# Four buffers of split weights moved to 0, 32, 64 and 192 bytes past a multiple of 256

## What is computed

```python
proj = jnp.einsum('bsd,dc->bsc', h, w_in)                    # first layer, 3420 columns
x = x + jnp.einsum('bsc,cd->bsd', mixed, w_out)
# two layers of the second kind
h = rms_norm_2(x) * (1 + sc_m) + sh_m
proj = h @ w_in                                              # 3520 columns
x = x + g_m * (y @ w_out)
gate, up = jnp.split(h @ w_ffn_in, 2, axis=-1)               # 1024 -> 2 x 2816
x = x + g_f * ((jax.nn.silu(gate) * up) @ w_ffn_out)         # 2816 -> 1024
```

## Time and profile before

| | |
|---|---|
| median of three runs | 1832.57 us |
| the profiled execution, whole | 1833.59 us |
| its span, first to last instruction | 1831.4 us |
| TensorE busy with matmuls | 1759.6 us (96%) |
| TensorE loading weights | 1424.0 us (78%) |
| VectorE, ScalarE, GpSimd busy | 965.0, 724.1, 686.1 us |
| mean granted TensorE clock | 0.988 |
| DMA, share of 16 engines | 31.4% |

### The profile page before, as it was taken

How to read it: one execution, slowest core, us unless ns; L and a number is a source line. 1 busy time by engine, 2 the same in 40 slices (tenths; PEclk the granted TensorE clock), 3 DMA queues, 4 the chain that set the end, 5 groups by cost and what they waited for, 6 DMA issues and landing times. The chain is left out here.

```text
span 1831.4 us, 23403 instructions
## 1 busy us (share of the span) xinstructions
PE 1759.6 (96%) x8343; PEld 1424.0 (78%) x8349; DVE 965.0 (53%) x1746; ACT 724.1 (40%) x1244; POOL 686.1 (37%) x303
## 2 busy tenths in 40 slices
PE   6999999988999999999999999999999999999997
PEld 6877777777888766788888887888766788888886
DVE  7989688575579577633333322579665321101112
ACT  5434555623375554332213222466454232213221
POOL 2424111235430333554555555450211454444442
PEclk9999999999999999999999999999999999999998
DMA  6234001044332224355555532232211233232211
GB/s 244 81 104 138 24 25 35 24 166 135 113 104 99 76 80 137 128 207 184 185 189 201 184 139 92 81 115 93 103 35 35 69 104 101 83 106 101 93 58 47
DMA packets 56634, 197.67 MB, mean 108 GB/s; under 512 B 6993, under 2 KB 8017, under 8 KB 56530
## 3 DMA queue, kind: packets, MB, share of 16 engines
q1 hardware_dynamic: 56530, 196.26, 31.4%
HBM read 194.14 MB, written 2.10 MB: 107 GB/s over the span
## 5 line engine op out<-in xcount | busy, mean ns | idle before, releaser
L496 POOL TENSOR_TENSOR WL<-RAW,WH 128x1024 fp32r<-128x1024 f32 x234 | 590.7, 2529 | 907.7 <-ACT WH L585 568.0
L1743 PE MATMUL bank<-HH,WH 128*128 128x512 f32 x1120 | 437.0, 390 | 7.8 <-POOLq L501 5.8
L1745 PE MATMUL bank<-HH,WL 128*128 128x512 f32 x1120 | 435.9, 389 | 0.0
L1744 PE MATMUL bank<-HL,WH 128*128 128x512 f32 x1120 | 435.8, 389 | 0.0
L585 ACT ACTIVATE WH<-RAW 128x1024 fp32r<-128x1024 f32 x259 | 270.6, 1051 | 243.1 <-PE bank L1745 218.0
L1743 PEld LDWEIGHTS bank<-HH,WH 128*128 128x128 f32 x1120 | 210.2, 188 | 53.5 <-issue 10.1
L1745 PEld LDWEIGHTS bank<-HH,WL 128*128 128x128 f32 x1120 | 210.2, 188 | 43.8
L1744 PEld LDWEIGHTS bank<-HL,WH 128*128 128x128 f32 x1120 | 210.3, 188 | 43.1
L1676 DVE TENSOR_TENSOR HF<-SILU,bank 128x512 f32<-128x512 f32 x44 | 30.3, 688 | 314.2 <-PE bank L1745 311.2
L1743 PE MATMUL bank<-HDH,WH 128*128 128x512 f32 x352 | 137.1, 389 | 0.0
L1745 PE MATMUL bank<-HDH,WL 128*128 128x512 f32 x352 | 136.9, 389 | 0.0
(11 more groups left out here) (363 smaller groups left out, 2871.1 us busy)
## 6 DMA issues: line engine op xcount, KB each, us to landing
RAW<-in_stream SPq DMA_DIRECT2D x363, 512.0 KB, 3.3
out_t<-YA SPq DMA_DIRECT2D x8, 256.0 KB, 2.2
X<-in_xt SPq DMA_DIRECT2D x3, 512.0 KB, 8.7
X<-in_xt SPq DMA_DIRECT2D x2, 256.0 KB, 3.9
RAW<-in_stream SPq DMA_DIRECT2D x2, 256.0 KB, 4.2
ACC<-in_pos SPq DMA_DIRECT2D x1, 256.0 KB
gains<-in_gains SPq DMA_DIRECT2D x1, 224.0 KB
CS<-in_cs SPq DMA_DIRECT2D x1, 128.0 KB
```

The source lines that it names most:

```text
L496: nc.gpsimd.tensor_tensor(lo(k)[:], raw(k)[:], hi(k)[:].bitcast(F32), ALU.subtract).then_inc(sem["passed"], mark("passed", *k))
L1743: nc.tensor.matmul(out, A[0], B[0], start=first, stop=False)
L1744: nc.tensor.matmul(out, A[0], B[1], start=False, stop=False)
L1745: return nc.tensor.matmul(out, A[1], B[0], start=False, stop=last)
```

## The change

The four buffers of `WH` and of `WL` are moved up by 0, 32, 64 and 192 bytes. The small constants behind them move up by 192. To make room, `ones` shrinks from 128 to 64 columns (only 64 are ever read), and its load shrinks with it; so `ident` lies 192 bytes further on and all that follows `ones` 64 bytes further down. `W0` is rounded up to a multiple of 256 and comes out at the same 108 KB + 7936 bytes as before. `X`, `HH`, `HL`, `RAW` and everything in the work area stay where they were. No instruction is added, removed or moved on any engine, and no wait changes; the one instruction that differs in shape is the load of `ones` (128x64 in place of 128x128).

```diff
 SPLIT_RING = 4
+RING_SHIFT = (0, 32, 64, 192)
...
-        WH = [at(f"WH{i}", [P, 1024], F32R, (split0 + 8 * i) * KB) for i in range(SPLIT_RING)]
-        WL = [at(f"WL{i}", [P, 1024], F32R, (split0 + 4 + 8 * i) * KB) for i in range(SPLIT_RING)]
-        cur = [(split0 + 8 * SPLIT_RING) * KB]
+        WH = [at(f"WH{i}", [P, 1024], F32R, (split0 + 8 * i) * KB + RING_SHIFT[i]) for i in range(SPLIT_RING)]
+        WL = [at(f"WL{i}", [P, 1024], F32R, (split0 + 4 + 8 * i) * KB + RING_SHIFT[i]) for i in range(SPLIT_RING)]
+        cur = [(split0 + 8 * SPLIT_RING) * KB + RING_SHIFT[-1]]
...
-        ones = small("ones", [P, P], F32)
+        ones = small("ones", [P, 2 * NCMP], F32)
...
-        W0 = (cur[0] + 63) // 64 * 64 + 128
+        W0 = (cur[0] + 255) // 256 * 256
...
-            for dst, name in ((ones, "ones"), (ident, "ident")):
-                sp.dma_start(dst[:], a[name]).then_inc(sem["norm_consts"], mark("norm_consts", by=16))
+            sp.dma_start(ones[:], a["ones"][:, 0:2 * NCMP]).then_inc(sem["norm_consts"], mark("norm_consts", by=16))
+            sp.dma_start(ident[:], a["ident"]).then_inc(sem["norm_consts"], mark("norm_consts", by=16))
```

## The result

The changed kernel takes 1853.5 us (median of four runs, 1853.3 to 1858.2) against 1832.6 before, 20.9 us more; the ratio is 1.0139 with a 95% interval of 1.0120 to 1.0159. So it is slower, by nearly twice what I had forecast (11.9 us), and inside the range. The profiled execution is one of 1853.5 us with a span of 1851.3.

The account below looks back on a forecast made before the run. TensorE's matmul pace was taken to bound the kernel. To the median of 1832.6 us, 11.9 us was added for re-settling at slot passages, all other parts 0, giving 1844.5 us; the 8-in-10 range was 1808 to 1866.

Parts of the forecast that it names:

- The bounds: Per matmul in the shifted buffers: at best 10 ns less, 44 us in all; at worst 9 ns more, 40 us.
- the 13.3 ns: Each fp32r matmul of 512 columns at full clock: time above the 213.3 ns that its columns alone take.
- If the pace has to settle again each time and then reaches 227: At each of 259 passages between weight slots: settling again costs 0.046 us, 11.9 us in all; chance 0.27.
- The third rival: Slower in shifted buffers: never settling, 4.6 ns a matmul, 1853 us, or one notch higher, 6.7 ns, 1862 us; chance 0.22.
- faster: In shifted buffers a distance avoids one encounter of both streams, saving 6.7 ns a matmul; 1803 to 1828 us; chance 0.28.
- same: The matmul surcharge arises whatever the distance between weight load and moving stream; time stays at 1832.6 us; chance 0.23.
- The prediction's second place: The skill's rule for the distance of matmuls at full clock, N/2.4 + 2.5 ns, 215.8 here.

## Why the prediction was wrong

What bounds the kernel was read rightly: TensorE's pace went to the end, 22.7 us busy for 19.9 us of span, and the suppliers had room.

The bounds were right: the worst settled pace (234.3) and the best (226.7) lie inside the -10 to +9 ns taken from the earlier trace rows. That the pace depends on how weight load and stream lie to each other was right too. Whether the 13.3 ns that are left at distance 0 also come from that is not shown.

The step that failed is "If the pace has to settle again each time and then reaches 227". I read in the earlier trace rows that the pace is a settled state with an approach, and took it for granted that every distance has the same settled state. That put the change of the settled pace at nothing without a row for it. It is not nothing: with all buffers at 64, where nothing is left to settle, it is 233.3. And the approach itself was sized too large: 46 ns was the one at the start of a stage, behind matmuls of another kind; at a passage it is 30 ns into buffer 0 and 8 on average. Two errors of opposite sign: 2.1 us in place of 11.9 for the passages, and 23.0 in place of 0 for the settled paces. The third rival had it nearly whole, "settles one notch higher", 6.7 ns; its sum of 1862 took all three buffers at that notch, and buffer 3 is at a third of it. That its other sum, 1853 for a pace that never settles, is the measured time is luck: every buffer settles. Nor was the forecast the likeliest case by its own chances (0.27 against 0.28 for faster); it stood between the others.

The rival "same" falls with the all-64 kernel, and "faster" with the list of offsets: of the eight tried, 0 is the best at 512 columns. Its argument, that streams which start together at equal offsets must collide more, has the sign wrong there. The argument for a notch higher ("all paces on the way in but one or two are above 227") was the best evidence in the trace, and I should have given it more than 0.22: it says that 227 is at the low end of the paces seen, reached at one distance, and no row showed that another distance has it too.

The Trainium skill's page "SBUF — State Buffer", section "Who interferes with whom", has TensorE wait for nobody and its two read ports independent. The runs differ: moving the weights by 64 against the stream costs 6.7 ns a matmul, moving both costs nothing. No row speaks against the rule between engines (the dense windows of the earlier trace rows keep their pace at DMA shares from 0.26 to 0.69), but between TensorE's own load and its stream in fp32r at full clock it does not hold. The prediction's second place, "TensorE: Matmul & The Clock Gate", section "Back-to-back issue gap" of the Trainium skill, is only part of what that section says. It calls N/2.4 + 2.5 the gap of an isolated matmul and gives about 131 ns for a stream of weight loads and matmuls at 512 columns. Here the bf16 matmuls of line 1863 start 216 ns apart at full clock, the formula's value, and nothing of 512 columns settles below that.

What stays open is the mechanism below that: how the reads of a load and of a stream meet in the memory. The runs show that it depends on the distance modulo 256, that costs do not add up load by load, and that the load's own walk is not needed for a loss. Why 0 and 192 are better than the rest they do not show, nor what picks one pace where a distance has several.

## What to carry to other kernels

Where fp32r matmuls of 512 columns run back to back at full clock, place both operands of each, and all parts of a triple, at the same offset modulo 256 bytes; any other multiple of 32 cost 1.0 to 3.4% of the pace here (at 448 columns the distance 64 was the better one), and nothing warns of it, since neither waits nor other engines show it. Read the distance of starts in a dense stretch, compare it with columns / 2.4 GHz, and see whether it is one steady number. A steady number in a trace belongs to the conditions of that trace: before reckoning with it elsewhere, ask which row shows it under the new ones.

## What the runs showed of the hardware that was not expected

The settled paces lie on a grid of 6.667 ns, which is 16 columns at full clock. 226.67 and 233.33 ns are 34 and 35 steps, and the 448-column matmuls at offset 64 have 200.0, 30 steps. Others come to whole steps over a short cycle: 228.9 is 103 steps over three matmuls (offset 192), 234.3 is 246 over seven (96), and 128 has 70 over two (229 and 238 ns in turn) or 244 over seven.

A distance can have more than one settled state. The clearest case is that of the 448-column groups, one in each of the two later layers. In the kernel before both go at 202.7 ns. In the one with everything moved by 64, and in the one with only the constants moved, the distances are the same, and the first group has 202.7 and the second 206.7 throughout. PE's timeline of the kernel with everything moved, fifteen matmuls apart in each group:

```profile
454.86 0.36 PE L1743 MATMUL bank<-WH,HH 128*128 128x448 f32 x1
457.90 0.36 PE L1743 MATMUL bank<-WH,HH 128*128 128x448 f32 x1
...
1152.48 0.37 PE L1743 MATMUL bank<-WH,HH 128*128 128x448 f32 x1
1155.58 0.37 PE L1743 MATMUL bank<-WH,HH 128*128 128x448 f32 x1
```

That is 3.04 and 3.10 us for the same fifteen distances. With all buffers at 64 these matmuls have 200.0, better than at 0 (192 matmuls, half a microsecond in all), here ten apart:

```profile
450.08 0.36 PE L1745 MATMUL bank<-WL,HH 128*128 128x448 f32 x1
...
452.08 0.36 PE L1746 MATMUL bank<-WH,HL 128*128 128x448 f32 x1
```

The experiments above have three more cases at 512 columns: 128, with 233.3 and 232.4; 192 in the token-major form, with 228.9 and 233.3; and the mixed triple of `HDH` and `HDL`. Where the distance stayed the same from slot to slot, the pace changed only between stages, behind a pause or behind a stretch at half clock, and then held. So a pace read in one stage need not be that of the next, even at the same distance. At distance 0 and 512 columns the triples came back to 226.7 behind such pauses too.

No version tried has a shorter time than the kernel before: the two that tie with it (1.0005 and 1.0006) leave the distances as they were.
